# Seven products for half of the gate units of two MLPs, and two more direct units ahead of a feed-forward's first run

## The reference, cut to what matters

```python
def swiglu(h, w_in, w_out):
    a, b = jnp.split(h @ w_in, 2, axis=-1)
    return (jax.nn.silu(a) * b) @ w_out

# second block, layer i, after its mixer m
h = layer_norm(DN_ALPHA * x + m, ln1_g[i], ln1_b[i])
f = jnp.square(jax.nn.relu(h @ mlp_w1[i])) @ mlp_w2[i]
e = jax.nn.sigmoid(h @ ple_w_gate[i]) * (p[i] @ ple_w_proj[i])
x = layer_norm(DN_ALPHA * h + f + e, ln2_g[i], ln2_b[i])
```

## Time and profile before

| | before |
|---|---|
| three runs, us | 2626.52, 2630.25, 2632.18 (median 2630.25) |
| profiled execution, us | 2629.4, span 2627.6 |
| mean granted TensorE clock | 0.997 |
| PE, PEld busy | 98 %, 82 % |
| DVE, ACT, POOL busy | 53 %, 45 %, 41 % |

### The profile page before, as it was taken

The page is one execution under the profiler, slowest core; times in us unless marked ns, Lnnn a source line. Parts: engine busy times, 40 slices in busy tenths (PEclk is TensorE's granted clock), DMA queues, the critical chain, the costliest instruction groups (busy, mean ns, idle before and its releaser), DMA issues.

```text
span 2627.6 us, 40349 instructions
## 1 busy us (share of the span) xinstructions
PE 2569.7 (98%) x15940; PEld 2160.0 (82%) x15940; DVE 1388.7 (53%) x2479; ACT 1192.8 (45%) x2071; POOL 1076.0 (41%) x501
## 2 busy tenths in 40 slices
PE   8999999999999999999999999999999999999998
PEld 6887788888777777899977678899887778889997
DVE  4566543343533338353658857455445564744554
ACT  4454422222543345453543845445445774534543
POOL 2222343443323324464633634555542112555552
PEclk9999999999999999999999999999999999999999
DMA  8622244543222211232232022323331112232332
GB/s 325 239 97 96 96 161 151 198 160 114 92 73 73 73 65 58 83 118 94 96 100 96 18 73 93 100 87 99 112 105 61 45 49 73 87 103 86 104 103 82
DMA packets 49843, 271.62 MB, mean 103 GB/s; under 512 B 5583, under 2 KB 9319, under 8 KB 25608
## 3 DMA queue, kind: packets, MB, share of 16 engines
q1 hardware_dynamic: 45648, 265.71, 29.4%
q10 hardware_dynamic: 4024, 3.54, 0.6%
HBM read 267.09 MB, written 2.13 MB: 102 GB/s over the span
## 4 chain that ended last, share of the span: by engine, by line
PE 68%; issue 22%; POOL 5%; DVE 3%; ACT 1%; POOLq 0%; ACTq 0%; DVEq 0%
PE lin L879 14%; PE lin L881 13%; PE lin L880 13%; PE lin L1959 6%; PE lin L1960 6%; PE lin L1961 6%; POOL wlo L756 5%; PE lin L1431 2%; PE bank L1415 1%; PE bank L1449 1%; PE bank L1610 1%; PE bank L1028 0%; PE lin L1435 0%; PE bank L1602 0%; PE lin L1602 0%
## 5 line engine op out<-in xcount | busy, mean ns | idle before, releaser
L756 POOL TENSOR_TENSOR wlo<-raw,whi 128x1024 fp32r<-128x1024 f32 (+4 forms) x202 | 696.9, 3450 | 1309.7 <-ACT whi L2101 1309.7
L2101 ACT ACTIVATE whi<-raw 128x1024 fp32r<-128x1024 f32 (+4 forms) x202 | 295.4, 1462 | 601.1 <-PE lin L881 541.6
L879 PE MATMUL lin<-hhi,whi 128*128 128x512 f32 x1160 | 465.4, 401 | 7.4 <-issue 2.6
L881 PE MATMUL lin<-hhi,wlo 128*128 128x512 f32 x1160 | 453.3, 391 | 0.0
L880 PE MATMUL lin<-hlo,whi 128*128 128x512 f32 x1160 | 452.4, 390 | 0.0
L879 PE MATMUL lin<-ghi,whi 128*128 128x512 f32 x1136 | 445.8, 392 | 2.5 <-ACT m L2121 1.7
L881 PE MATMUL lin<-ghi,wlo 128*128 128x512 f32 x1136 | 442.3, 389 | 0.0
L880 PE MATMUL lin<-glo,whi 128*128 128x512 f32 x1136 | 442.2, 389 | 0.0
L777 POOL TENSOR_TENSOR wlo<-raw,whi 128x512 fp32r<-128x512 f32 x200 | 265.9, 1343 | 174.4 <-ACT whi L2433 172.2
L879 PEld LDWEIGHTS lin<-hhi,whi 128*128 128x128 f32 x1160 | 218.2, 188 | 68.6 <-issue 14.9
L881 PEld LDWEIGHTS lin<-hhi,wlo 128*128 128x128 f32 x1160 | 218.0, 188 | 47.1
(11 more groups left out here) (538 smaller groups left out, 4400.6 us busy)
## 6 DMA issues: line engine op xcount, KB each, us to landing
raw<-in_w SPq DMA_DIRECT2D x139, 1024.0 KB, 4.9
raw<-in_w SPq DMA_DIRECT2D x85, 512.0 KB, 3.6
adw_a<-in_ada SPq DMA_DIRECT2D x30, 1024.0 KB, 5.0
adw_b<-in_ada SPq DMA_DIRECT2D x18, 1024.0 KB, 5.5
raw<-in_w SPq DMA_DIRECT2D x12, 768.0 KB, 5.6
raw<-in_w SPq DMA_DIRECT2D x8, 640.0 KB, 3.9
raw<-in_w SPq DMA_DIRECT2D x8, 384.0 KB, 3.1
x<-in_x SPq DMA_DIRECT2D x1, 2048.0 KB, 9.8
```

Source lines behind the costliest of these rows:

```text
L756: nc.gpsimd.tensor_tensor(wlo[:, slot, 0:size], raw[:, slot, 0:size], whi[:, slot, 0:size].bitcast(F32), ALU.subtract).then_inc(s.wlo_ok, 1)
L879: pe.matmul(dst, lh, rh, start=first, stop=False)
L881: return pe.matmul(dst, ll, rh, start=False, stop=last)
L2101: act.activation(whi[:, slot, 0:size], raw[:, slot, 0:size], ACT.Copy).then_inc(s.whi_ok, 1)
```

## The change

Two of the four gate units of each MLP become seven-product units (`gate_seven`) and join the MLP's first run, which now has six units. Their four quarters get the sigmoid in PSUM, and DVE multiplies them straight into `m`. The input sums, the first unit's weight sums and its first blocks now stand between the four remaining gate tiles. In the second feed-forward, six direct units stand ahead of a run of two. POOL's `input_sums` is gone: DVE adds all eight chunks in one instruction. In the first feed-forward, SP issues the loads of units 26 and 27 (and 28/29, 32) ahead of the `ada` pair that stood before them.

```diff
-        single = 4 if k == 0 else 0
+        single = 6 if k == 0 else 0
...
-    mlp = [("ple", 2, 1024)] + [("gate", DC, 256)] * 4
+    mlp = [("ple", 2, 1024)] + [("gate", DC, 256)] * 2
+    mlp += [("gate_seven", DC, 256)] * 2
...
             for u in range(26, min(34, len(plan))):
-                if u in (26, 28, 32):
-                    ada_pair({26: 32, 28: 34, 32: 36}[u])
                 next_unit(u, plan[u][1] * plan[u][2])
+                if u in (27, 29, 32):
+                    ada_pair({27: 32, 29: 34, 32: 36}[u])
...
@@ POOL
-            def input_sums(u):
-                for c in range(4):
-                    pool.wait_ge(s.h_ok, FFN_H + c + 1)
-                    nc.gpsimd.tensor_tensor(m[:, c, :], hhi[:, c, :].bitcast(F32), hlo[:, c, :].bitcast(F32), ALU.add)
...
@@ PE, mlp and ffn_short
-                lin_loop(4, hin, s.h_ok)
+                lin_loop(2, hin, s.h_ok)
...
-                    seven_run(4, 1 + i if part == 0 else None)
+                    seven_run(4 if part else 6, None if part else 1 + i)
...
                 lin_pair(hin, s.h_ok, (5, 6))
+                lin(2, hin)
-                seven_run(4, 0)
+                seven_run(2, 0)
...
@@ ACT, seven_run: a gate unit
+                    if u < h0:
+                        act.activation(A[:, half0], A[:, half0], ACT.Sigmoid).then_inc(s.part_ok, 1)
+                        ahead(3, 4)
...
+                        act.activation(U[:, half0], U[:, half0], ACT.Sigmoid).then_inc(s.part_ok, 1)
...
@@ ACT, mlp
-                for k in range(8):
+                for k in range(4):
                     act.wait_ge(s.mm, n.up(s.mm))
-                    if k in (1, 3):
-                        split_next()
                     bank = LB[(tile[0] + k) % 4][:, :]
                     act.activation(bank, bank, ACT.Sigmoid).then_inc(s.gate_ok, 1)
-                    if k == 3:
+                    if k == 1:
                         combined_high(1 + i)
-                    for j in {5: (0, 1, 2, 3), 7: (4, 5, 6)}.get(k, ()):
+                    for j in {1: (0, 1, 2, 3), 3: (4, 5, 6)}.get(k, ()):
                         block_high(st.u + 2, j)
...
@@ DVE, ffn_short
-                v.wait_ge(s.m_ok, HAD["m_ok"] + 4)
-                combined_sums(0, m, second_half)
+                v.wait_ge(s.h_ok, n.at(s.h_ok))
+                chain(v.tensor_tensor(m[:, :, :], hhi[:, :, :].bitcast(F32), hlo[:, :, :].bitcast(F32), ALU.add))
+                combined_sums(0, m)
                 single(0)
...
@@ DVE, mlp
-                for k in range(8):
+                for k in range(4):
                     n.up(s.mm)
                     v.wait_ge(s.gate_ok, n.up(s.gate_ok))
+                    if k == 0:
+                        combined_sums(1 + i, x)
                     v.tensor_tensor(m[:, k, :], LB[(tile[0] + k) % 4][:, :], projected[:, k, :], ALU.mult)\
                         .then_inc(s.ev_d, 1)
                     n.up(s.ev_d)
                     if k == 1:
-                        combined_sums(1 + i, x)
-                    if k == 4:
-                        for j in range(4):
+                        seven_sums(u)
+                        for j in range(2):
                             combined_low(1 + i, j)
-                    next_run(u, k)
+                            block_low(u, j + 1)
+                        combined_low(1 + i, 2)
+                        combined_low(1 + i, 3)
+                    elif k == 3:
+                        block_low(u, 5)
```

More of the change, by code:

```diff
@@ L142, in stop_units @@
         if first:
-            while u < len(PLAN) and PLAN[u][0] in (last, "ffn_in", "mlp_in", "ffn_seven", "mlp_seven"):
+            while u < len(PLAN) and PLAN[u][0] in (last, "ffn_in", "mlp_in", "ffn_seven", "gate_seven", "mlp_seven"):
                 u += 1
@@ L803, in all_lows @@
                         continue
-                    v = u + 1
-                    while v < last and v not in ORDINAL and v + 1 != SEVEN[0]:
+                    v = u
+                    while v < last and v not in ORDINAL:
                         v += 1
@@ L2445, in seven_run @@
                 u0, per = st.u, 2 if rectified else 1
+                h0 = min(u for u in range(u0, u0 + count) if PLAN[u][0] != "gate_seven")
                 def hidden_high(u, which):
-                    g, c = ORDINAL[u], chunk0 + per * (u - u0) + which
+                    g, c = ORDINAL[u], chunk0 + per * (u - h0) + which
                     if rectified and which == 0:
@@ L2535, in ffn_short @@
                 silu_pair(tile[0], 0)
+                split_next()
                 combined_high(0)
+                silu_pair(tile[0], 1)
+                split_next()
+                tile[0] += 4
+                silu_pair(tile[0], 0)
                 for k in range(4):
@@ L3496, in combined_sums @@
                 v.tensor_tensor(tsum[:, 0, :, :], quarter(0, half1), quarter(0, half0), ALU.subtract).then_inc(s.t_sum, 1)
-                if other is not None:
-                    other()
                 v.wait_ge(s.t_sum, HAD["t_sum"] + 4 * stage + 1)
@@ L3516, in seven_run @@
                 parts = 4 * (base - FFN_SEVENS) + FFN_SEVENS if rectified else base
-                highs = 2 * (base - FFN_SEVENS) + FFN_SEVENS if rectified else base
+                gates = sum(PLAN[u0 + i][0] == "gate_seven" for i in range(count))
+                highs = 2 * HIDDEN[u0 + gates] + FFN_SEVENS if rectified else base
                 def times(dst, bank, factor, done):
@@ L3538, in seven_run @@
                     ahead(1, 2)
-                    if rectified:
+                    k = 4 + 2 * i
+                    if i < gates:
+                        v.wait_ge(s.part_ok, HAD["part_ok"] + parts + 4 * i + 1)
+                        times(m[:, k, half0], A, projected[:, k, half0], s.a_free)
+                    elif rectified:
                         v.wait_ge(s.part_ok, HAD["part_ok"] + parts + 4 * i + 1)
@@ L3546, in seven_run @@
                     v.tensor_tensor(V[:, half0], V[:, half0], p5, ALU.add).then_inc(s.c12_ok, 1)
-                    if rectified:
+                    if i < gates:
+                        v.wait_ge(s.part_ok, HAD["part_ok"] + parts + 4 * i + 3)
+                        times(m[:, k, half1], V, projected[:, k, half1], s.first_ok)
+                        times(m[:, k + 1, half1], Q, projected[:, k + 1, half1], s.q_free)
+                        v.wait_ge(s.part_ok, HAD["part_ok"] + parts + 4 * i + 4)
+                        times(m[:, k + 1, half0], U, projected[:, k + 1, half0], s.u_free)
+                        ahead(5)
+                    elif rectified:
                         v.wait_ge(s.part_ok, HAD["part_ok"] + parts + 4 * i + 3)
```

73 lines of the change are left out of this document (39 added, 34 removed).

## The result

| | before | after |
|---|---|---|
| median of the runs, us | 2632.18 (9 runs, 2626.52 to 2633.48) | 2639.21 (9 runs, 2636.51 to 2640.74) |
| profiled execution, span, us | 2627.6 | 2638.9 |
| mean granted TensorE clock | 0.997 | 0.994 |
| PE, DVE, ACT, POOL busy | 98 %, 53 %, 45 %, 41 % | 98 %, 53 %, 45 %, 41 % |

The ratio is 1.0024, 95% interval [1.0016, 1.0033]: 7.0 us slower, where 7.7 were forecast. The median lies 1.2 us from the predicted 2638, which was counted from the first three runs of before; from the median of all nine, 2632.18, the forecast of +7.7 would be 2639.9.

What follows compares the result with a forecast made beforehand. PE, busy 98% of the span, was taken to bound the kernel. First feed-forward -1.9, second -2.4 and MLPs +12.0 sum to +7.7 us on 2629.4: 2637.1, or 2638 against the median; range 2627 to 2643.

Steps and rivals of the forecast that it cites:

- Units: Whole kernel: each unit moved from direct to seven products gives back 0.83 us; net -1.7 us over MLPs and feed-forward.
- First feed-forward: SP's load order: PE's 1.75 us wait for unit 28's weights and the restart behind it go, -1.9 us.
- Second feed-forward: Four waits go, a 3.8 us wait for DVE's eviction comes before the fifth direct unit; -2.4 us taken.
- its bound of -1.7: Second feed-forward: gain of only 1.7 us if the clock falls behind the 3.8 us wait.
- The MLPs: Each first run: PE waits 6.2 us at the third product, plus 1.5 us of clock, less cheaper units: +6.0 us.
- DVE's own queue: MLPs: DVE's work ahead of the last `m` and the seed alone makes PE wait 2.6 us at the third product.
- the lock: MLPs: POOL's instructions shut DVE out of the four `tlo`, which lose 3.6 us together.
- The other term: MLPs: the clock falls behind the 6.2 us wait, costing 1.5 us in each MLP.
- A: Rival, whole change: DVE and POOL don't meet, evictions are timely, feed-forward waits go; -12.4 us, 2618; chance 0.10.
- its own point: MLPs, sign of the result: a third-product wait under about 3.5 us with its clock loss makes the whole change faster.
- B: Rival, MLPs: last `m` late only by DVE's own work, 2.6 us, clock stays up; total -3.5 us, 2627; chance 0.18.
- C: Rival, MLPs: U-to-V seed waits for two more evictions, clock down for two stretches; 3 us an MLP, 2644; chance 0.12.

Runs made afterwards that it cites:

- both orders together: Changed kernel with the feed-forward's third direct unit evicted ahead of the four `tsum`, and each MLP's `tsum` ahead of the first gate wait; 0.9996 of before.
- the experiment on ACT's order: Changed kernel with both reorderings and POOL behind the `tlo`, plus ACT's feed-forward combined highs behind its second silu pair and next weight split; 2622.04 us, 0.9958 of before.
- the version with the sums first: Changed kernel with the four `tsum` of each MLP ahead of DVE's wait for the first gate tile; 2633.84 us, 1.0006 of before.

## Why the prediction was right

**Units.** 0.83 us a unit held: six seven-product units would be 60.5 us, and the runs without a slow stretch lie above it by their waits and little else (62.3 with 1.4 us).

**First feed-forward.** Forecast -1.9, measured -1.91, and in the experiment with that edit alone the wait went and none took its place.

**Second feed-forward.** The wait in front of the fifth unit was 3.25 for a forecast 3.8, ended by the instruction named. The four waits of the earlier trace rows were gone. But the clock did fall behind the wait, a case which the prediction had as its bound of -1.7: the stretch gave -1.80. I had weighed that case by six tenths into the -2.4; the row that should have counted more was the earlier trace rows, a fall behind 2.42 us. A wait of 0.5 us inside the run of two, for DVE's `lin` L3556, is there too, against the "no more" of the prediction.

**The MLPs.** The mechanism was right, and both halves of it have an experiment of their own: DVE's order (moving `tlo` behind the `m` moves the wait) and POOL's lock (POOL behind the `tlo` takes 2.1 us off). The size was 6.2 for 4.86. Of the 1.3 us, 0.7 is DVE's own queue (1.9 for 2.6: the four `tsum` alone ran 0.4 us shorter than laid out by hand) and 0.65 the lock (2.95 for 3.6). Beside it stands that ACT wrote the block for POOL's third `wlo` only behind the fourth gate tile, so that POOL was idle for 0.84 us in the middle; that this made the lock smaller isn't tested. The other term was too small: 1.5 us for the clock, for 2.0 and 2.7 as estimated from the trace, because the slow stretch was twice as long as the one in the earlier trace rows. The two errors cancel in part, and that is luck: +5.10 and +5.67 for +6.0.

**The rivals.** A wanted waits under 3.5 us and fails by its own point. B, DVE's own queue only, fails as a forecast of after, but the experiment with POOL behind the `tlo` comes near to B made true: a wait of 2.77, of which 0.9 is still lock, and a kernel that can't be told from before (0.9998), one slow stretch included. C had the right clock, down for 6.8 us behind both waits, and the wrong reason and size: the seed of the second gate unit waited for nothing.

**What failed in the expectations.** The order of the feed-forward's eviction alone gave 2 us where about 5 were expected. The step left out was the cast: I had taken from the rows that only instructions with two SBUF inputs are locked out, and `CAST ghi<-sq` has one. By the page SBUF — State Buffer of the Trainium skill, section "Who interferes with whom", a cast can enter a two-port mode in which it contends with GpSimd like the others, and the row of 4.52 us agrees. The prediction's short form of that rule, by which an instruction with at most one SBUF input goes free, left this case out; in its own chain, of `tensor_tensor` alone, it makes no difference. The wait through ACT was the second step left out, and the experiment on ACT's order showed it. The two expectations built on it, 0.997 for both orders together and 0.9953 with POOL moved as well, failed with it (0.9996 and 0.9972).

## What to carry to other kernels

When a cheaper form of a unit takes the place of a dearer one that stood ahead of it, ask first how much cover the dearer one gave to the preparation: here 21.8 us of direct work less turned 3.3 us of gain into two waits of 4.9 us. List each engine's queue over that cover, put first what releases banks, put nothing that doesn't need the gate behind the wait for it, and look whether VectorE and GpSimd meet on it. And follow a wait that you remove one engine further than the one you moved: it came back through ScalarE and GpSimd.

## What the runs showed of the hardware

- VectorE and GpSimd lock each other out for whole instructions, in both directions, and the price is what is left of the other's instruction: `tsum` 1.22 to 5.51 us beside a POOL instruction of 5.28, a one-input cast from 0.42 to 4.52 beside one of 4.60, POOL's `wlo` from 1.30 to 1.99 beside `tlo`. `wlo<-bank,whi`, with one operand in PSUM, stayed at 0.68 in after at 1602.57, while POOL's `wlo` of 1601.83 to 1603.82 was under way.
- The clock's fall behind a wait is no function of the wait's length alone. Behind 2.77 us it fell in one MLP and not in the other of the same execution; behind the 1.41 us of the MLPs and the 1.75 us of the earlier trace rows it did not fall; behind the 1.81 us in the feed-forward with its eviction first it did, and in before it fell at 1353.55, between waits of 1.14 and 0.85 us. Behind waits of about 4.85 us it stayed down for 6.8 us instead of 3.4; behind one of 3.25 us in the second feed-forward it did so too in the version with the sums first, and not in after. A stretch of 3.4 us costs 1.5 us as measured (POOL behind the `tlo`) and 1.7 us by the prediction's estimate from the earlier trace rows. Such stretches also stand in places that the edits do not touch, in one trace and not in another, and make a part of the spread of the times; why they fall where they do stays open.
